# Sums of squares as two rounded products in place of one fp32 product, and query roots one tile earlier

## The reference

```
l2_normalize(q), l2_normalize(k)   # x * rsqrt(sum(x*x, -1) + 1e-6), 8 heads of 64, first layer
_rms_norm(c_q, ...), _rms_norm(c_kv, ...)   # 256 latent features each, last two layers
k = _rms_norm(k, k_head_g)         # 8 heads of 96, the 64 that have no rotation come from k_nope
```

## Time and profile before

| | |
|---|---|
| median of 3 runs | 2028.53 us (2026.54 to 2028.76) |
| the profiled execution | 2024.96 us, of it 2023.2 us span |
| TensorE busy | 2001.9 us, 99% |
| DVE, ACT, POOL busy | 63%, 52%, 35% |
| chain that ended last | TensorE 93%, DVE 3%, ACT 2%, DMA 1% |
| TensorE waits for others | 7.8 us once for POOL, 4.1 us once for ACT, under 2 us each elsewhere |

### The profile page before, as it was taken

The page is one execution under the profiler, slowest core; times in us unless marked ns, Lnnn a source line. Parts: engine busy times, 40 slices in busy tenths (PEclk is TensorE's granted clock), DMA queues, the critical chain, the costliest instruction groups (busy, mean ns, idle before and its releaser), DMA issues.

```text
span 2023.2 us, 31697 instructions
## 1 busy us (share of the span) xinstructions
PE 2001.9 (99%) x12708; PEld 1672.2 (83%) x12708; DVE 1274.9 (63%) x2266; ACT 1050.5 (52%) x1743; POOL 717.5 (35%) x354
## 2 busy tenths in 40 slices
PE   8999999999999999999999999999999999999999
PEld 6877878888988887778889888878789987878997
DVE  6885566566656347873665655558777733777672
ACT  7742365344436327883644434556764443767441
POOL 3332134444444630003444443444024444412443
PEclk9999999999999999999999999999999999999999
DMA  4442123232332431002233333222023322211232
GB/s 161 132 123 73 58 88 105 97 106 100 105 104 84 141 105 37 12 2 98 94 104 105 104 98 102 83 95 93 12 63 105 105 94 94 83 33 53 94 106 93
DMA packets 62736, 179.28 MB, mean 89 GB/s; under 512 B 17776, under 2 KB 18160, under 8 KB 62592
## 3 DMA queue, kind: packets, MB, share of 16 engines
q1 hardware_dynamic: 47600, 168.04, 25.2%
q10 hardware_dynamic: 14992, 9.22, 1.7%
HBM read 171.97 MB, written 3.70 MB: 87 GB/s over the span
## 4 chain that ended last, share of the span: by engine, by line
PE 93%; DVE 3%; ACT 2%; DMA 1%; issue 1%; ACTq 0%; POOL 0%; DVEq 0%
PE banks L942 20%; PE banks L943 19%; PE banks L944 19%; PE banks L1044 6%; PE banks L1045 6%; PE banks L1043 6%; PE banks L1426 2%; PE banks L1447 2%; PE banks L1411 2%; PE banks L1536 1%; PE banks L1549 1%; PE banks L1521 1%; PE banks L993 1%; PE banks L1527 1%; PE banks L1319 1%
## 5 line engine op out<-in xcount | busy, mean ns | idle before, releaser
L3372 POOL TENSOR_TENSOR w_lo<-raw,w_hi 128x1024 fp32r<-128x1024 f32 (+4 forms) x350 | 717.3, 2056 | 1289.6 <-ACT w_hi L1694 1133.9
L1694 ACT ACTIVATE w_hi<-raw 128x1024 fp32r<-128x1024 f32 (+2 forms) x274 | 263.8, 964 | 419.0 <-PE banks L944 296.6
L942 PE MATMUL banks<-h_lo,w_hi 128*128 128x512 f32 (+1 forms) x800 | 325.6, 407 | 7.9 <-POOL w_lo L3372 7.8
L942 PE MATMUL banks<-a_lo,w_hi 128*128 128x512 f32 x832 | 329.3, 396 | 0.0
L943 PE MATMUL banks<-a_hi,w_lo 128*128 128x512 f32 x832 | 324.4, 390 | 0.0
L944 PE MATMUL banks<-a_hi,w_hi 128*128 128x512 f32 x832 | 324.0, 389 | 0.0
L944 PE MATMUL banks<-h_hi,w_hi 128*128 128x512 f32 (+1 forms) x800 | 313.3, 392 | 0.0
L943 PE MATMUL banks<-h_hi,w_lo 128*128 128x512 f32 (+1 forms) x800 | 313.0, 391 | 0.0
L2532 DVE TENSOR_TENSOR x<-x,banks 128x512 f32<-128x512 f32 x168 | 115.1, 685 | 213.4 <-PE banks L944 213.4
L942 PEld LDWEIGHTS banks<-h_lo,w_hi 128*128 128x128 f32 (+1 forms) x800 | 150.3, 188 | 46.6 <-POOL w_lo L3372 7.8
L942 PEld LDWEIGHTS banks<-a_lo,w_hi 128*128 128x128 f32 x832 | 156.1, 188 | 39.2 <-DVE x L2532 7.3
(11 more groups left out here) (470 smaller groups left out, 4148.9 us busy)
## 6 DMA issues: line engine op xcount, KB each, us to landing
raw<-in_weights SPq DMA_DIRECT2D x311, 512.0 KB, 3.3
x<-in_x SPq DMA_DIRECT2D x4, 512.0 KB, 5.7
AT<-row_dram ACTq DMA_DIRECT2D x4, 512.0 KB, 9.4
out<-x SPq DMA_DIRECT2D x8, 256.0 KB, 2.0
eg<-row_dram ACTq DMA_DIRECT2D x8, 128.0 KB, 3.0
phase<-in_phase ACTq DMA_DIRECT2D x1, 706.0 KB, 3.9
phase<-in_phase ACTq DMA_DIRECT2D x1, 704.0 KB, 4.0
ld_dram<-Ld ACTq DMA_DIRECT2D x1, 512.0 KB, 6.6
```

What stands on the lines that cost most here:

```text
L942: mm(out, w_hi, x_lo, start=first, stop=False)
L1694: ins = f(c.w_hi[:, b % RING, cols], c.raw[:, b % RING, cols], ACT.Copy)
L3372: return nc.gpsimd.tensor_tensor(c.w_lo[:, slot, to], c.raw[:, slot, first:end], c.w_hi[:, slot, to].bitcast(F32), ALU.subtract)
```

## The change

Each of 24 sums of squares (8 `l2`, and 4 latent and 4 key sums in each of two layers) is now made of two rounded matmuls: `sq_hi` (the square, rounded) and `sq_lo` (what the rounding left), both by a rounded copy of the mask. ACT squares the source twice, into `sq` and into `sq_hi`; POOL subtracts, in `sq`'s own place; TensorE waits for POOL. POOL does its subtraction ahead of the weight block that was next when ACT wrote the square. Three masks are rounded once by ACT. The sums 2 and 3 of the queries are both at (16, 4), and ACT and DVE take the roots of queries 0 and 1, and ACT the squares 2 and 3, at tile 13 and no longer at 14.

```diff
-    (13, 4): [("l2", 0), ("l2", 1)], (16, 0): [("l2", 2)], (16, 4): [("l2", 3)],
+    (13, 4): [("l2", 0), ("l2", 1)], (16, 4): [("l2", 2), ("l2", 3)],
-ROOTS_AT = {4: (4, 1), 6: (6, 3), 14: (0, 5), 17: (2, 7)}
+ROOTS_AT = {4: (4, 1), 6: (6, 3), 13: (0, 5), 17: (2, 7)}
...
+    def sum_rounded(key, over, n=1):
+        out = claim(key)
+        for k in range(n):
+            slot = sums[0] % 2
+            pe.wait_ge(c.sq_lo_ready, rounded_sums[0] + 1)
+            mm(out[:, :], over, c.sq_hi[:, slot, :], start=k == 0, stop=False)
+            mm(out[:, :], over, c.sq_lo[:, slot, :], start=False, stop=k == n - 1).then_inc(c.sq_used, 1)
...
-                    sum_squares(key, k0["blk64"])
+                    sum_rounded(key, c.blk64_r[:, :])
...
-                        sum_squares(("lat", l, which), ones, 2)
+                        sum_rounded(("lat", l, which), c.ones_r[:, :], 2)
...
         if l == 0:
             pe.wait_ge(c.phase2_loaded, 16)
+            pe.wait_ge(c.masks_rounded, 3)
         for h in range(6):
...
             if 2 <= h < 6:
-                sum_squares(("hs2", l, "k", h - 2), k2["blk64_2"])
+                sum_rounded(("hs2", l, "k", h - 2), c.blk64_2_r[:, :])
...
+    def square_parts(src):
+        i = count["sq"]
+        f(square_buffer(i, c.sq_used, i + 1), src, ACT.Square)
+        f(c.sq_hi[:, i % 2, :], src, ACT.Square).then_inc(c.sq_ready, 1)
+        squares_behind.append((count["w"], i))
...
-        if t in (14, 17):
+        if t in (13, 17):
             head_roots(ROOTS_AT[t][0], ROOTS_AT[t][0] + 1)
-        if t == 14:
+        if t == 13:
             head_square(2)
             head_square(3)
...
         passed("kn", l, 3)
+        if l == 0:
+            act.wait_ge(c.phase2_loaded, 16)
+            f(c.blk64_2_r[:, :], c.phase2[...], ACT.Copy).then_inc(c.masks_rounded, 1)
...
+            def square_low(i):
+                pool.wait_ge(c.sq_ready, i + 1)
+                nc.gpsimd.tensor_tensor(c.sq_lo[:, i % 2, :], c.sq[:, i % 2, :], c.sq_hi[:, i % 2, :].bitcast(F32), ALU.subtract)\
+                    .then_inc(c.sq_lo_ready, 1)
             for b in range(n_blocks):
+                for behind, i in squares_behind:
+                    if behind == b:
+                        square_low(i)
                 pool.wait_ge(c.w_hi_ready, b + 1)
```

More of the change, by code:

```diff
@@ L649, in place @@
     c.rstd, at = put("rstd", [P, 2, T], at)
+    c.sq_hi, _ = put("sq_hi", [P, 2, T], c_stage, F32R)
+    c.sq_lo, _ = put("sq_lo", [P, 2, T], at, F32R)
     c.sq, at = put("sq", [P, 2, T], at)
@@ L654, in place @@
     at = aligned(at + 4 * max(PHASE_N, PHASE0_N + 2 * T))
+    c.blk64_r, _ = put("blk64_r", [P, P], phase + 4 * PHASE0["blk64"][0], F32R)
+    c.blk64_2_r, _ = put("blk64_2_r", [P, P], phase + 4 * PHASE2["blk64_2"][0], F32R)
     c.phase0, _ = put("phase0", [P, PHASE0_N], phase)
@@ L840, in add_semaphores @@
     c.sq_used = sem("sq_used")
+    c.sq_lo_ready = sem("sq_lo_ready")
+    c.masks_rounded = sem("masks_rounded")
     c.norm_sq = sem("norm_sq")
@@ L985, in token_major @@
                 beside(k)
+    rounded_sums = [0]
+    def sum_rounded(key, over, n=1):
[5 more added lines that the diff above has]
+            mm(out[:, :], over, c.sq_lo[:, slot, :], start=False, stop=k == n - 1).then_inc(c.sq_used, 1)
+            sums[0] += 1
+            rounded_sums[0] += 1
     def sum_squares(key, over, n=1, rows=P):
@@ L1490, in query_sums @@
                 pe.wait_ge(c.sq_ready, at + 1)
-                over, h0, n = (k2["blk32_4"], 4 * i, 4) if i < 2 else (k2["blk64_2"][:, 0:P:64], 2 * (i - 2), 2)
+                over, h0, n = (k2["blk32_4"], 4 * i, 4) if i < 2 else (c.blk64_2_r[:, 0:P:64].bitcast(F32), 2 * (i - 2), 2)
                 for qt in range(NT):
@@ L1664, in source_numbers, with program_scalar @@
     return {key: n for n, key in enumerate(k for k in split if k[0] == "cn")}
-def program_scalar(act, nc, c, block, bank, split, beside, early, n_blocks, sums):
+def program_scalar(act, nc, c, block, bank, split, beside, early, n_blocks, sums, squares_behind):
     f = nc.scalar.activation
@@ L1760, in square @@
         f(square_buffer(i, c.sq_used, i + 1)[0:rows, :], src, ACT.Square).then_inc(c.sq_ready, 1)
+        count["sq"] += 1
+    def square_parts(src):
[3 more added lines that the diff above has]
+        squares_behind.append((count["w"], i))
         count["sq"] += 1
@@ L1927, in program_scalar @@
     weights(3)
+    act.wait_ge(c.common_loaded, 16)
+    f(c.ones_r[:, :], c.common[:, P:2 * P], ACT.Copy).then_inc(c.masks_rounded, 1)
+    act.wait_ge(c.phase0_loaded, 16)
+    f(c.blk64_r[:, :], c.phase0[:, PHASE0["blk64"][0]:PHASE0["blk64"][0] + P], ACT.Copy).then_inc(c.masks_rounded, 1)
     norm_root(0)
@@ L1932, in program_scalar @@
     step(f(c.e_row[ab, :], c.e_row[ab, :], ACT.Exp, scale=-1.0))
-    f(c.e_row[ab, :], c.e_row[ab, :], ACT.Ln, bias=c.common[ab, P:P + 1]).then_inc(c.g_ln_ready, 1)
+    f(c.e_row[ab, :], c.e_row[ab, :], ACT.Ln, bias=c.ones_r[ab, 0:1].bitcast(F32)).then_inc(c.g_ln_ready, 1)
     def head_roots(*tiles):
@@ L1948, in head_square @@
         read(("qkv", i))
-        square(c.qkv[:, i, :])
+        square_parts(c.qkv[:, i, :])
     def beside_tile(t):
@@ L2239, in program_scalar @@
             read((("cq", "ckv")[i // 2], l, i % 2))
-            square(c.c[:, i, :])
+            square_parts(c.c[:, i, :])
         passed("uf", l, 2)
@@ L2250, in program_scalar @@
         passed("kn", l, 3)
+        if l == 0:
+            act.wait_ge(c.phase2_loaded, 16)
+            f(c.blk64_2_r[:, :], c.phase2[:, PHASE2["blk64_2"][0]:PHASE2["blk64_2"][0] + P], ACT.Copy).then_inc(c.masks_rounded, 1)
         for i in range(6):
@@ L2256, in program_scalar @@
                 read(("kn", l, i - 1))
-                square(c.kn[i - 1])
+                square_parts(c.kn[i - 1])
         for i in range(2):
@@ L3366, in _ @@
             sp.wait_ge(c.out_written, 16 * KT)
+        squares_behind = []
+        @blocks.scalar
+        def _(act):
+            program_scalar(act, nc, c, block, bank, split, beside, early, n_blocks, sums, squares_behind)
         @blocks.gpsimd
@@ L3383, in _ @@
                 ins.then_inc(c.w_lo_ready, 1)
-        @blocks.scalar
-        def _(act):
-            program_scalar(act, nc, c, block, bank, split, beside, early, n_blocks, sums)
         @blocks.vector
```

12 lines of the change are left out of this document (8 added, 4 removed).

## The result

| | before | changed |
|---|---|---|
| median of 8 runs | 2026.36 us (2023.74 to 2028.76) | 2037.39 us (2033.99 to 2043.88) |
| ratio | | 1.0052, 95% interval 1.0043 to 1.0061 |
| the profiled execution | 2024.96 us | 2038.71 us, of it 2036.9 us span |

A forecast was written before the change was run, and what follows sets the result against it. TensorE, busy 2001.9 of 2023.2 us, was taken as the bound. Terms -2.4 + 2 x 1.4 + 1.8 + 2 x 3.5 = +9.2, with one clock fall +11.6: 2036.6 profiled, 2039.5 as median; range 2032 to 2047.

The forecast's parts named there:

- the first layer: Up to the first use of the inverse at tile 20: 2.4 us gained, bounds 1.0 to 5.
- the mask: First of the last two layers: query tiles wait until ACT has rounded blk64_2, +1.8 us once.
- the clock: Low clock behind the new waits: one fall at 2.4 us likeliest; bounds none, or four, 9.6 us.
- the keys: Key sums of the last two layers: waits 5.3 us less 1.6 saved, +3.5 us a layer.
- The long wait: At (16, 0) TensorE's 4.12 us wait for ACT's square and the low clock behind it go: 6.7 us together.
- The chain through POOL: At each sum, ACT's second square and POOL's subtraction let it start about 1.9 us later after the same square.
- the latents: Latent sums of the last two layers: waits of 0.6, 1.85 and 0.85 against 1.9 saved, +1.4 us a layer.
- that transfer is now issued 1.04 us later, behind two more squares: First layer: the triangles' DRAM transfer, and so DVE's elimination and its read for kt in tile 20, come later.
- the stall forecast at tile 16: First layer: the weight block's low part is done at 117.4, TensorE arrives at 114.9; a stall of 1.8 us.
- the other three: First-layer stalls at key sums (3, 2) and (3, 6) and tile 13's weight block: 1.3, 0.9 and 1.6 us.
- rival 4: Clock falls at most clusters of waits, four or more times: +19 us, 2047; 17 in 100.

The follow-up runs named there:

- move alone: Kernel before plus only the move of query roots and squares to tile 13 and both query sums to (16, 4), all sums fp32: ratio 0.9990, median 2023.82.
- kernel without low parts: Changed kernel, but in the last two layers TensorE multiplies sq_hi twice and POOL subtracts nothing, so norms there are wrong: ratio 0.9980.
- the kernel with SP's wait and kt later: Kernel before plus query move, SP loading weight block 17 only after Ld's store, first kt and vt at (20, 4); fp32 sums: ratio 0.9978, median 2021.65.

## Why the prediction was right, and where its terms were not

**The total**: +11.6 forecast for the profile, +13.7 measured; without the stretch from 160 to 900 us, 10.0. As a median +11 forecast, +11.0 measured. It is right mostly by its mechanism and partly by luck, since errors cancel: the first layer and the mask were forecast 3.1 us too dear, the clock 1.2, the keys 0.3 and the stretch from 160 to 900 us 3.75 too cheap.

**The long wait**: 6.7 forecast, 6.6 measured (move alone, 110-130). Right.

**The chain through POOL**: right. Waits at the keys (second layer) 1.94, 0, 1.35, 1.50 against 1.9, 0, 1.5, 1.9; at the latents 0.28, 1.73, 0.43 against 0.6, 1.85, 0.85. +1.4 a layer forecast for the latents, 1.39 and 1.44 measured where the clock does not fall; +3.5 for the keys, 3.63. The kernel without low parts shows that POOL's step makes the loss: the doubled squares alone only use up the saving.

**The step that failed** is in the first layer: "that transfer is now issued 1.04 us later, behind two more squares". It was issued at 96.77, before at 96.68. DVE had the last of `Ld` ready only at 96.65 before and at 96.74 now, so ACT's squares weren't what it waited for. And it landed after 4.5 us instead of 6.6, because POOL's two subtractions held back SP's weight load. DVE's elimination began at 106.61, 0.4 earlier than before (107.00) and not 1.04 later. From this came the rest: ACT, released earlier, had its roots begun at 103.33 and the block of tile 16 copied at 110.23 where I had 113.2, so the stall forecast at tile 16 (1.8) did not come (the other three came at 1.0, 0.6 and 1.5, forecast 1.3, 0.9 and 1.6); DVE's reader stood at 145.12 and not at 146.6 (146.6 less the 1.04 that did not come and the 0.4 gained is 145.2), y5 at 148.57 and not at 150.0. Measured: -3.7 for the layer (3.88 less the 0.21 of the start), forecast -2.4, inside the bounds of 1 and 5.

**The mask**: +1.8 forecast, nothing measured. ACT rounds it at 1351.58, and TensorE needs it at 1355.94.

```profile
1351.58 0.29 ACT L2291 ACTIVATE blk_r<-phase 128x128 fp32r<-128x128 f32 x1
```

I had taken the wrong row: the weight block ahead of the mask is one earlier than that of 1353.53 in the earlier trace rows.

**The clock**: one fall at 2.4 us forecast; three at 3.6 together. 2.4 was read behind the earlier trace rows, where the low level lasted from 118.0 to 124.8; behind these waits it lasts half as long. So rival 4 had the number nearly right (three of four clusters) and the price wrong. The Trainium skill (TensorE: Matmul & The Clock Gate, A second HAM failure mode) states that short idle times between groups of matmuls are enough to make the clock swing. The trace agrees in part: no new wait was over 1.94 us and the clock fell to 0.50 three times, but not behind the same 1.94 us at the keys of the second layer.

**The sum by its terms**: -3.7 + 2.8 + 0 + 7.3 + 3.6 = +10.0, forecast -2.4 + 2.8 + 1.8 + 7.0 + 2.4. The remaining 3.8 lie between 160 and 900 us, 3.6 of them in the attention at 780.

**What stays open** is that stretch. The prediction has no term for it. Of the twelve profiles other than before's, four have a low clock there for some 10 us, four a shorter one and four none, whatever they changed, and the instructions there are those of before; the kernel with SP's wait and kt later has such a fall at 198 us as well (its +6.64). It follows no edit, so I count it to none; what starts it was not tried. The times suggest that such falls come and go from one execution to the next: the kernel without low parts took 2019.8 us in one at a mean clock of 1.000 and 2025.6 in its profiled one at 0.997. Each kernel has one trace only, so where its other executions lost their time isn't shown.

Nor is it known which wait brings a fall. With the same waits the clock fell at the keys of the first of the last two layers, but not of the second, in the changed kernel; with rounded sums in the last two layers alone it was the other way round. At kt it fell behind waits of 1.9 and 2.8 us, and not behind those of 2.1 to 2.6.

## What to carry to other kernels

A cheaper product on the engine that sets the pace is worth something only if its operand is ready: count the new chain behind the operand (here 0.52 + 1.3 us on two other engines) against the distance that the old one had, and move the consumer back in the same edit. When a transfer's landing sets a chain, look at what else is issued with it; one wait in SP's queue, on top of the query move, gave here as much as any version with all 24 rounded sums. And read the price of a low clock for each wait where it falls, not from the longest one.

## What the runs showed of the hardware that was not expected

A 512 KB store to DRAM landed after 6.6 us when a 512 KB load was issued 0.08 to 0.11 us before it (three profiles), and after 4.5 or 4.6 us when the load came 1.4 us or more behind it (ten profiles). The clock that TensorE is granted differs between profiles in stretches where the kernels have the same instructions, and one such stretch (776 to 787 us at 0.53) moved a profile by 3.6 us, as much as the first layer's whole gain; a difference of that size needs the medians, or the lag stretch by stretch.
